# Streamed weight strips in the ring of picked rows: one buffer fewer, ten slots in place of nine

## What is computed

```python
def block(xb):                                   # 128 tokens
    q = (xb @ w_q).reshape(BLK, PEER_HEADS, PEER_QDIM)
    ...
    v1, i1 = lax.top_k(s1, K)
    v2, i2 = lax.top_k(s2, K)
    ...
    sc, ci = lax.top_k(cand, K)
    e = ...                                      # 8 x 16 experts for each token
    g = jax.nn.softmax(sc, axis=-1)
    ue = u[e]
    ve = v[e]
    a = jax.nn.gelu(jnp.einsum('thkd,td->thk', ue, xb), approximate=False) * g
    return jnp.einsum('thk,thkd->td', a, ve)
```

## Time and profile before

| | |
|---|---|
| median of 3 runs | 2904.25 us (2898.63 to 2904.93) |
| the profiled execution | 2902.58 us |
| its span, first to last instruction | 2900.4 us |
| TensorE matmuls busy | 2284.9 us, 79% |
| VectorE busy | 2184.6 us, 75% |
| ScalarE, GpSimd busy | 41%, 43% |
| DMA | 1170.27 MB, mean 403 GB/s |

### The profile page before, as it was taken

The page is one execution under the profiler, slowest core; times in us unless marked ns, Lnnn a source line. Parts: engine busy times, 40 slices in busy tenths (PEclk is TensorE's granted clock), DMA queues, the critical chain, the costliest instruction groups (busy, mean ns, idle before and its releaser), DMA issues.

```text
span 2900.4 us, 27200 instructions
## 1 busy us (share of the span) xinstructions
PE 2284.9 (79%) x7394; PEld 1213.3 (42%) x7394; DVE 2184.6 (75%) x5166; ACT 1183.7 (41%) x3457; POOL 1244.1 (43%) x1049
## 2 busy tenths in 40 slices
PE   9779787788877887786887878877788878886567
PEld 8536442454424554243443434443354434432122
DVE  2688678876878757796688876988679876887664
ACT  3154334344343443445344453435534453433333
POOL 0254335443444333444434543354434444345655
PEclk9899999899999898998899988989889998988989
DMA  6599999999999999999999999999999999999998
GB/s 271 209 418 421 398 398 416 421 421 403 415 420 421 420 375 420 420 418 421 421 393 406 422 421 420 389 416 421 421 402 406 421 421 421 399 421 421 422 422 350
DMA packets 170817, 1170.27 MB, mean 403 GB/s; under 512 B 19668, under 2 KB 19928, under 8 KB 36136
## 3 DMA queue, kind: packets, MB, share of 16 engines
q0 software_dynamic: 147456, 1073.81, 89.7%
q1 hardware_dynamic: 23208, 94.74, 8.3%
HBM read 1164.28 MB, written 4.19 MB: 403 GB/s over the span
## 4 chain that ended last, share of the span: by engine, by line
DMA 28%; DVE 14%; PE 11%; issue 6%; POOL 3%; ACT 3%; POOLq 0%; DVEq 0%; ACTq 0%
DMA ring<-in_uv,pick 26%; PE acc L1723 6%; DVE ring L1094 4%; POOL ring L666 3%; PE ps L1514 3%; DVE side L1085 1%; DMA xc<-h 1%; DMA stream<-in_strips 1%; ACT diag L1368 1%; DVE arena L969 1%; DVE arena L950 1%; DVE arena L1040 1%; DVE arena L1044 1%; DVE arena L951 1%; DVE arena L1031 1%
## 5 line engine op out<-in xcount | busy, mean ns | idle before, releaser
L666 POOL DMA_INDIRECT ring<-in_uv,pick x1024 | 1239.7, 1211 | 1630.5 <-PE acc L1723 1092.9
L1723 PE MATMUL acc<-ring,diag 128*128 128x512 f32 x2988 | 1542.5, 659 | 465.3 <-ACT diag L1368 462.3
L1094 DVE CUSTOM_DVE_ANT_0 ring<-ring,h_now 128x1024 f32<-128x1024 f32 x1024 | 1235.4, 1222 | 490.2 <-DMA ring<-in_uv,pick 474.0
L1723 PEld LDWEIGHTS acc<-ring,diag 128*128 128x128 f32 x2988 | 582.6, 207 | 1287.7 <-ACT diag L1368 702.8
L1357 ACT ACTIVATE gelu<-dots 128x1 f32<-128x1 f32 x1024 | 206.1, 201 | 1264.6 <-DVE dots L1094 1258.0
L1085 DVE SCALAR_TENSOR_TENSOR side<-ring,coef,side 128x1024 f32<-128x1024 f32 x270 | 346.0, 1281 | 23.1 <-ACT coef L1360 23.0
L1360 ACT ACTIVATE coef<-gate,gelu 128x1 f32<-128x1 f32 x1024 | 302.0, 295 | 33.2
L1368 ACT ACTIVATE diag<-ident,coef 128x128 f32<-128x128 f32 x747 | 300.1, 402 | 29.8 <-PE acc L1723 5.5
L1514 PE MATMUL ps<-resident,actT 128*128 128x256 f32 x896 | 220.3, 403 | 14.5 <-ACT actT L1169 14.5
L1514 PEld LDWEIGHTS ps<-resident,actT 128*128 128x128 f32 x896 | 178.1, 202 | 58.9 <-issue 18.2
L1481 PE MATMUL ps<-actT,stream 128*128 128x128 f32 x960 | 124.9, 291 | 23.6 <-DMA stream<-in_strips 22.7
(11 more groups left out here) (198 smaller groups left out, 1454.6 us busy)
## 6 DMA issues: line engine op xcount, KB each, us to landing
stream<-in_strips SPq DMA_DIRECT2D x102, 512.0 KB
resident<-in_strips SPq DMA_DIRECT2D x18, 1024.0 KB, 12.9
ring<-in_uv,pick POOLq DMA_INDIRECT x1024
ring<-in_strips SPq DMA_DIRECT2D x9, 1024.0 KB, 19.6
arena<-in_keys SPq DMA_DIRECT2D x8, 512.0 KB
xc<-in_x SPq DMA_DIRECT2D x4, 512.0 KB
h<-arena SPq DMA_DIRECT2D x4, 512.0 KB, 11.4
xc<-h SPq DMA_DIRECT2D x4, 512.0 KB
```

The lines of the kernel that those rows point to most:

```text
L666: pool.indirect_dma_start(ring[:, n % SLOTS, :], None, tables[layer], bass.IndirectOffsetOnAxis(ap=pick[:, col:col + 1], axis=0),).then_in ...
L1094: dve.tensor_tensor_reduce(ring[:, slot, 0:D], ring[:, slot, 0:D], h_now[:], 1.0, 0.0, ALU.mult, ALU.add, dots[:, slot:slot + 1]).then_inc ...
L1723: m = pe.matmul(acc[:, b * 512:(b + 1) * 512], diag[:, turn % 4, :], ring[:, slot, D + b * 512:D + (b + 1) * 512], start=(r == 0 and i == ...
```

## The change

The buffer `stream` is gone. `ring` has ten slots of 1 MB. A table `PLACE` gives each pick and each streamed strip a place in one sequence: the strip that TensorE uses at beat b stands ahead of pick b - 1. The place modulo ten is its slot. SyncE loads a whole strip into its slot once the item ten places earlier has been used (L558 of the changed kernel), GpSimd does the same for picks, and TensorE frees a strip's slot with its last matmul.

Which strips stream is changed as well. `KEPT` holds nine strips a layer in `resident`: in layer 0 q1, k1, v3, r3, out3 and the four pq; in layer 1 q1, q3, kv, out2, out3 and the four pq. The others pass through the ring for every block: 11 in layer 0 (q0, k0, v0 to v2, r0 to r2, out0 to out2), 4 in layer 1 (q0, q2, out0, out1). Of the kept strips of layer 1, four and not five are loaded ahead in stage 2, and five in stage 3. In the opening the first ten passing strips fill the ten slots. `AT` and `VECTOR` are unchanged.

```diff
-SLOTS = 9
+SLOTS = 10
...
-RESIDENT = 9
+KEPT = ((1, 3, 7, 11, 15, 16, 17, 18, 19), (1, 3, 4, 7, 8, 9, 10, 11, 12))
+RESIDENT = len(KEPT[0])
...
-AHEAD, AHEAD_AT, REST_AT = 5, 10, 5
+AHEAD, AHEAD_AT, REST_AT = 4, 10, 4
...
+def ring_order():
+    order = [(0, 0, n) for n in PASSING[0]]
+    for s in range(STAGES):
+        layer, p = divmod(s + 1, BLOCKS)
+        at = AT["first" if s == 0 else "gla" if layer == 0 else "swa"]["pe"]
+        for i in range(PICKS):
+            if s + 1 < STAGES:
+                order += [(layer, p, n) for n in PASSING[layer] if at[PIECES[layer][n]] - 1 == i]
+            order.append(s * PICKS + i)
+    return {item: place for place, item in enumerate(order)}
...
-        stream = sb("stream", [P, KT, STRIP])
...
         def released(eng, n):
-            eng.wait_ge(used[n % SLOTS], n // SLOTS + 1)
+            eng.wait_ge(used[slot_of(n)], turn_of(n) + 1)
+
+        def emptied(eng, item):
+            if turn_of(item):
+                eng.wait_ge(used[slot_of(item)], turn_of(item))
...
+            def load_passing(prep, n):
+                item = (prep.layer, prep.p, n)
+                emptied(sp, item)
+                sp.dma_start(ring[:, slot_of(item), :], strips[prep.layer][n])\
+                  .then_inc(strip_got[slot_of(item)], 16)
...
             def load_streamed(prep):
                 if prep.layer == 1:
+                    for n in PASSING[1]:
+                        if n < out0(prep):
+                            load_passing(prep, n)
+                    if prep.first:
+                        load_kept_rest(prep)
                     said_by(sp, "pe", prep, "o3")
                     sp.dma_start(bias_out, b_out).then_inc(bias_loaded, 16)
...
+                else:
+                    for n in PASSING[0][SLOTS if prep.first else 0:]:
+                        load_passing(prep, n)
+                said_by(sp, "pe", prep, "oT")
...
+                if prep.layer == 1:
+                    for n in PASSING[1]:
+                        if n >= out0(prep):
+                            load_passing(prep, n)
+                said_by(sp, "pe", prep, "y")
+                sp.dma_start(keysT, (keys0, keys1)[prep.layer]).then_inc(keys_loaded, 16)
...
-                    if n >= SLOTS:
-                        released(pool, n - SLOTS)
-                        alone(pool, passed["pool"])
...
+                    emptied(pool, n)
+                    alone(pool, passed["pool"])
```

More of the change, by code:

```diff
@@ L145, with slot_of, turn_of, landings @@
 }
+PIECES = (("q0", "q1", "k0", "k1", "v0", "v1", "v2", "v3", "r0", "r1", "r2", "r3", "out0", "out1", "out2", "out3",
+           "pq0", "pq1", "pq2", "pq3"),
+          ("q0", "q1", "q2", "q3", "kv", "out0", "out1", "out2", "out3", "pq0", "pq1", "pq2", "pq3"))
+def ring_order():
[8 more added lines that the diff above has]
+    return {item: place for place, item in enumerate(order)}
+PLACE = ring_order()
+def slot_of(item):
+    return PLACE[item] % SLOTS
+def turn_of(item):
+    return PLACE[item] // SLOTS
+def landings():
+    seen = {(kind, slot): 0 for kind in ("strip", "pick") for slot in range(SLOTS)}
+    count = {}
+    for item in sorted(PLACE, key=PLACE.get):
+        key = ("strip" if isinstance(item, tuple) else "pick", slot_of(item))
+        seen[key] += 1
+        count[item] = seen[key]
+    return count
+LANDED = landings()
 def opening(engine):
@@ L206, in value @@
         return self.p * len(names) + (base + names.index(event) + 1)
[L208 to L216, removed]
 def alone(eng, passed):
@@ L319, in build @@
         res_loaded = [sem(f"res_loaded{i}") for i in range(RESIDENT)]
[L320 to L322 removed]
+        strip_got = [sem(f"strip_got{s}") for s in range(SLOTS)]
         consts_loaded = sem("consts_loaded")
@@ L414, in before, with passing @@
             return Prep(prep.kind, prep.p - 1)
-        def in_ring(prep, n):
-            return prep.first and prep.layer == 0 and RESIDENT <= n < RESIDENT + SLOTS
+        def passing(prep, n):
+            return n in PASSING[prep.layer]
         def weight(prep, n):
[L422 to L426, removed]
+            if not passing(prep, n):
+                return resident[:, KEPT[prep.layer].index(n)]
+            return ring[:, slot_of((prep.layer, prep.p, n)), :].rearrange("p (k c) -> p k c", k=KT)
         def out0(prep):
@@ L533, in load_streamed @@
                     said_by(sp, "pe", prep, "o3")
                     sp.dma_start(bias_out, b_out).then_inc(bias_loaded, 16)
[L535 to L545, removed]
-                        sp.dma_start(ffn_gain, gain_ffn[prep.layer:prep.layer + 1, :]).then_inc(gain_loaded, 16)
-                    if n == KEYS_AT[prep.layer]:
-                        said_by(sp, "pe", prep, "y")
-                        sp.dma_start(keysT, (keys0, keys1)[prep.layer]).then_inc(keys_loaded, 16)
-                    for c in range(CUTS):
-                        if opening and n < SLOTS:
-                            break
-                        if n > (SLOTS if opening else 0):
-                            freed(prep, (n - 1) * CUTS + c)
-                        elif not opening:
-                            freed(before(prep), (STREAMED[before(prep).layer] - 1) * CUTS + c)
-                        sp.dma_start(stream[:, c * CUT:(c + 1) * CUT, :].rearrange("p k c -> p (k c)"),
-                                     strips[prep.layer][RESIDENT + n, :, c * CUT * STRIP:(c + 1) * CUT * STRIP])\
-                          .then_inc(slot_loaded[c], 16)
```

89 lines of the change are left out of this document (34 added, 55 removed).

## The result

The changed kernel takes 2908.91 us (median of 11 runs, 2906.78 to 2910.68) against 2901.04 (11 runs, 2896.98 to 2904.93) for the kernel before: a ratio of 1.0029, 95% interval 1.002 to 1.0038. The forecast was 2882 us, in a range from 2864 to 2901, with a chance of 0.8 for faster. The kernel is slower, and outside the range. The profiled execution has a span of 2906.8 us at a granted clock of 0.91 (0.915 before).

The account below looks back on a forecast made before the run. DMA was taken as the bound: bytes over rate plus stretches not fed. Late strips -17.5, opening -2.5 and layer 1 -2 gave -22 from 2902.58 us, 2880.6; with 1.7 for the median, 2882 us, range 2864 to 2901.

Parts of the forecast that it names:

- late strips in layer 0: Layer 0: strips issued ten places, about 25 us, before use always arrive in time, so waits for them go: -17.5 us.
- the three holes: Layer 0 stretches 350:450, 650:750 and 1000:1075, with 8.4, 4.2 and 7.9 us not fed, each to fall to about 1 us.
- third rival: Layer 0: the chain through VectorE and ScalarE also holds releases, holes stay but for a third; 2895 to 2901 us, chance 0.08.
- Layer 1, -2 us: Layer 1, VectorE-limited stretch for 1811:1892: lost filling offset by run-ahead, earlier releases and select steps; -0.5 a stage, four stages.
- my bounds of -5 to +6: Layer 1, us a stage: -5 if nearly all the hole closes, +6 if filling is lost and only the tenth pick runs ahead.
- the rival of the missed filling: Layer 1: ten slots are soon full while VectorE selects; +6 us in each of four stages, 2906 us, chance 0.12.
- The opening, -2.5 us: Start of the kernel: a tenth slot lets GpSimd issue a tenth pick before its first long stop, filling 2.5 us.
- New waits at nothing: Layer 1's out0 strip, layer 0's first strip of a stage and GpSimd's slot waits: covered or as before, no cost.
- The slower rival: Layer 1: out0's strip lands late and TensorE stalls 9 us in each of four stages; 2918 us, chance 0.07.
- 4 KB rows to 8 KB rows at nothing: Strip loads: whole strips in place of halves change row size; taken as no gain, with 16 us as upper bound.
- the bound of 0.16 us a half: Strip loads: most that each stream half could cost, from 420 against 422 GB/s in 450:650; 16 us for all 102.

Follow-up runs that it names:

- +4: Against the changed kernel, every passing strip stands four picks later in the ring's order, nothing else changed: 2899.22 us, ratio 0.9995.

## Why the prediction was wrong

- **The step that failed is the one on late strips in layer 0, -17.5 us.** "It should always be there", and the strips are: TensorE's waits for strips in layer 0 are nil. "I take each of the three holes to about 1 us, since nothing else in them is full" is what was wrong. Something else filled up once the strips moved in: the ring. I had worked out that a strip is issued ten places, 25 us, ahead against a landing of 9.2, and had read the 16 us between them as safety (the trace has 31 us for r0, since the slot comes free earlier than the place tells). They are 16 us in which a slot serves nobody (22 in the trace, for r0), three times over in a cluster, and GpSimd stops there. "GpSimd waits as before, on one slot for each pick. Both at nothing": it waited 182.7 us at strips, and the 7.86 us at r0's slot alone stand before 5.5 us of idle. Measured: +3.1 in place of -17.5 (layer 0's +1.4, less the opening's -1.7). That it is the hold and the clusters is shown by the runs with other places (-10, +105) and spread strips (-6), for the second and third stage; what the first keeps is open. The prediction's sign of its third rival, holes as large in layer 0 with no strip wait in them, came true, but that rival's mechanism (VectorE and ScalarE hold the releases) leaves no room for what spreading the strips took away.
- **Layer 1, -2 us.** Measured +8.2. The mechanism was written down ("7.5 us of filling leave a stretch that stays as long as VectorE makes it"), and then offset term by term with sizes of my own choice: 2.5 of run-ahead, 1.8 of earlier releases, 0.9, 0.8. In the 81 us that it worked out, 7.0 us of idle were priced; the changed kernel has 8.4 there (378 GB/s in 1819:1900). All four streamed strips of layer 1 were query strips; the three of the prediction are those loaded in rounds 12 and 13. The measured filling is 5.2 us a stage and what the tenth slot gives back is 3.2, so +2 a stage, within my bounds of -5 to +6. This was the rival of the missed filling, at 2 us a stage and not at 6, and its total of 2906 lay nearest to the result, by luck: it had layer 0 as the forecast had it.
- **The opening, -2.5 us.** Right in kind: GpSimd issues ten picks before it stops, for 13.8 us where 15.0 stood. The first two rounds have 2.2 us of idle in place of 3.9. The 1.7 us that went ahead of the first dot, and 2.1 at the end of the kernel, I had not counted; the kernel with nine slots has the end's gain too (5.7), so that one is not the tenth slot's. The tenth slot's worth, though, is that of the run with nine: 22 us, nearly all of it behind the opening.
- **New waits at nothing.** For out0's strip in layer 1, TensorE waits about 3.5 us a stage and not 0, so its waits for strips sum to 13.9 where under 10 were to show the forecast right. No idle follows: 1730:1800, which holds the wait of the fifth stage, runs at 421 GB/s. The slower rival, 9 us a stage and a load of 16 us, did not come: the loads land in 9.5. The result is slower, for another reason than this rival's.
- **4 KB rows to 8 KB rows at nothing.** Nothing speaks against it: whole strips in an own slot leave layer 1 at 26.8 us of idle, halves in the buffer of before at 26.3. With a scatter of up to 7 us between profiles this does not rule out the bound of 0.16 us a half, 5 us for layer 1's 32 halves. The Trainium skill's fit (DMA: Bandwidth & Descriptors, Anatomy of one DMA), given there for transfers that GpSimd issues, would have made these two differ by 2.0 us a strip, an estimate of 32 us for layer 1 if nothing overlapped. These two traces of SyncE's loads show no such difference.
- **The sum.** Forecast against its own execution -22, measured +6.4 in the span. Of the 28.4 between them 20.6 are the late strips, 10.2 layer 1, 0.8 the first two rounds, -2.1 the end and -1.7 what stands ahead of the first dot; 0.6 is left over.

## What to carry to other kernels

When a transfer moves into a shared ring whose slots are issued in order, price the whole time for which it takes its slot, issue to release, and count how many such items stand in the ring at once; lead beyond the landing time takes a slot for as long as it lasts (too little of it cost here as well, 44 us at seven picks later). Before taking away a separate buffer, ask which transfers it lets through while the ring is stopped by another engine, because only those fill such a stretch. A wait that disappears gives its time only if the resource behind it does not take its place, so look for what will be full after the change.

## What the hardware showed that I had not expected

A strip's load on SyncE's queue landed 9.5 us after its issue (median of 60) while the picks on GpSimd's queue took 16.2 (median of 1024) and the engines were at 420 GB/s: the 1 MB load is not queued behind all the picks issued before it. That fits with so late a place as +4 still working. The price of a slot is steep and not even: nine in place of ten +22 us, three picks of longer hold +105 us, against 10 us for four picks less.
